# X tiles loaded in one row, a reciprocal in the gate chain, and two forms of the first output row moved in a two-layer decoder kernel

## The reference

```python
y = rmsnorm(x, a_norm)
proj = y @ w_in                                   # q, k, v, o and 2*4 gate columns
gates = 15.0 * tanh((gates + b_gates) / 15.0)
ig, fg = split(gates)
lf = log_sigmoid(fg)
# per head, in chunks: b = cumsum(lf); D = b_t - b_s + ig_s; running maximum m
# num = (q k^T * exp(D - m)) v + exp(...) C q ; h = num / max(|den|, exp(-m))
x = x + (rmsnorm(h) * sigmoid(o)) @ w_out
x = x + swiglu(rmsnorm(x))                        # w_gate_up, w_down
# second layer: shared K/V, sliding-window attention with sinks, then swiglu; final rmsnorm
```

## Time and profile before

| | |
|---|---|
| median of three runs | 2072.8 us (2071.33 to 2073.25) |
| the profiled execution | 2074.34 us, its span 2072.7 us |
| PE busy in the span | 2019.2 us (97%) |
| DVE, ACT, POOL busy | 1349.9, 925.3, 1211.6 us |
| granted PE clock, mean | 0.994 |
| moved by DMA | 415.03 MB, 200 GB/s |

### The profile page before, as it was taken

How to read it: one execution, slowest core, us unless ns; L and a number is a source line. 1 busy time by engine, 2 the same in 40 slices (tenths; PEclk the granted TensorE clock), 3 DMA queues, 4 the chain that set the end, 5 groups by cost and what they waited for, 6 DMA issues and landing times.

```text
span 2072.7 us, 29248 instructions
## 1 busy us (share of the span) xinstructions
PE 2019.2 (97%) x9992; PEld 1660.2 (80%) x9992; DVE 1349.9 (65%) x1929; ACT 925.3 (45%) x1951; POOL 1211.6 (58%) x1058
## 2 busy tenths in 40 slices
PE   7899999999999999999999999899999999999998
PEld 6788989878888888888878666588788888888886
DVE  7654652668777777464665677768776676645567
ACT  6444343365545545432344444536545444432233
POOL 5532520664888988565664111264888797756565
PEclk9999999999999999999999999999999999999999
DMA  5655545843777787795844000564567667688673
GB/s 154 194 189 181 184 156 203 304 133 122 254 234 258 238 255 244 252 393 169 269 136 85 28 22 22 203 213 122 176 231 251 226 229 249 213 306 313 203 257 139
DMA packets 295431, 415.03 MB, mean 200 GB/s; under 512 B 40040, under 2 KB 218232, under 8 KB 295296
## 3 DMA queue, kind: packets, MB, share of 16 engines
q1 hardware_dynamic: 260752, 307.87, 45.3%
q10 hardware_dynamic: 33120, 100.68, 13.5%
q0 software_dynamic: 1424, 4.77, 0.8%
HBM read 259.09 MB, written 154.17 MB: 199 GB/s over the span
## 4 chain that ended last, share of the span: by engine, by line
PE 86%; DVE 7%; ACT 3%; issue 2%; DMA 1%; POOL 0%; SPq 0%; ACTq 0%; DVEq 0%; POOLq 0%
PE ps L2216 21%; PE ps L2218 21%; PE ps L2217 21%; PE ps L2119 8%; PE ps L2121 4%; PE ps L2480 1%; PE ps L2339 1%; PE ps L2340 1%; PE ps L2336 1%; PE ps L2271 1%; PE ps L2509 1%; DVE mats L1652 1%; PE ps L2499 1%; DVE forms L1750 1%; PE ps L2385 1%
## 5 line engine op out<-in xcount | busy, mean ns | idle before, releaser
L2216 PE MATMUL ps<-forms,mats 128*128 128x512 f32 x2016 | 789.6, 392 | 5.5 <-ACT part L1302 2.3
L2218 PE MATMUL ps<-forms,mats 128*128 128x512 f32 x2016 | 785.9, 390 | 0.0
L2217 PE MATMUL ps<-forms,mats 128*128 128x512 f32 x2016 | 785.8, 390 | 0.0
L1007 POOL TENSOR_TENSOR mats<-sum_a,mats 128x256 fp32r<-128x256 f32 (+2 forms) x384 | 405.6, 1061 | 365.4 <-ACT mats L1241 364.4
L2216 PEld LDWEIGHTS ps<-forms,mats 128*128 128x128 f32 x2016 | 379.4, 188 | 90.8 <-issue 10.2
L2218 PEld LDWEIGHTS ps<-forms,mats 128*128 128x128 f32 x2016 | 379.3, 188 | 79.2
L2217 PEld LDWEIGHTS ps<-forms,mats 128*128 128x128 f32 x2016 | 379.5, 188 | 77.6
L1675 DVE TENSOR_TENSOR X<-ps,X 128x512 f32<-128x512 f32 x390 | 268.4, 690 | 218.4 <-PE ps L2218 216.1
L1241 ACT ACTIVATE mats<-sum_a 128x256 fp32r<-128x256 f32 (+2 forms) x392 | 201.6, 516 | 324.0 <-PE ps L2218 306.7
L1652 DVE TENSOR_TENSOR mats<-stream_raw,mats 128x256 fp32r<-128x256 f32 (+2 forms) x302 | 277.1, 919 | 18.7 <-ACT mats L1241 18.0
L1241 ACT ACTIVATE mats<-stream_raw 128x256 fp32r<-128x256 f32 (+2 forms) x302 | 156.6, 519 | 249.6 <-PE ps L2218 246.1
(11 more groups left out here) (230 smaller groups left out, 2696.2 us busy)
## 6 DMA issues: line engine op xcount, KB each, us to landing
forms<-scratch_forms ACTq DMA_DIRECT2D x182, 512.0 KB, 5.4
scratch_forms<-prep_forms SPq DMA_DIRECT2D x161, 512.0 KB, 3.5
stream_raw<-in_w_gate_up_dram SPq DMA_DIRECT2D x88, 512.0 KB, 5.4
scratch_forms<-head_forms SPq DMA_DIRECT2D x49, 512.0 KB, 2.6
scratch_hidden<-hidden SPq DMA_DIRECT2D x84, 256.0 KB, 5.5
prep_raw<-in_w_down_dram SPq DMA_DIRECT2D x38, 512.0 KB, 5.7
stream_raw<-scratch_hidden SPq DMA_DIRECT2D x32, 512.0 KB, 4.6
forms<-scratch_forms SPq DMA_DIRECT2D x28, 512.0 KB, 8.1
```

The source lines that it names most:

```text
L1007: pool.tensor_tensor(blocks(m[:, q, 1, :], it.width), stream_source(it, q), blocks(m[:, q, 0, :].bitcast(F32), it.width), ALU.subtract).th ...
L2216: mm(dst, ah, bh, start=OPENS[q] and k == 0, stop=False, skip_group_check=True)
L2217: mm(dst, ah, bl, start=False, stop=False, skip_group_check=True)
L2218: m = mm(dst, al, bh, start=False, stop=k == w - 1, skip_group_check=True)
```

## The change

Three groups of edits, all in the first 130 us.

1. SP loads the eight x tiles in one row, and the norm's weights behind them. The two transfers of gate columns are issued by ACT's queue before its first instruction. The gate unit's split stands one tile earlier in the lists of ACT and DVE (behind tile 2's transposes in place of tile 3's).
2. In the gate chain, 1/u comes from a DVE reciprocal of 4x1024 in place of ACT's exp(-ln u). ACT scales the input gate, behind its logarithm and a one-column Exp that brings its table back. The hi part of head 0's unit 3 is made before the logarithm. POOL gains unit 4 behind the lo part of unit 3 and unit 5 behind the reload of the first row.
3. In head 0, ACT makes no form behind value copy 5; forms 5 and 6 of the first row stand behind copies 6 and 7, and the lo part of form 6 goes from before the chunk loop to its first turn.

```diff
@@ SP
-            for t in range(3):
+            for t in range(TT):
                 load_x(t)
-            sp.wait_ge(gate_w_cleared, 1)
-            ... (two gate column transfers)
-            load_gains(0, a_norm[0, :])
-            for t in range(3, TT):
-                load_x(t)
+            sp.dma_start(gcol[:, 0, :], a_norm[0, :].rearrange("(k p) -> p k", p=P), ...
+                         ).then_inc(a_gain_loaded, 16)
@@ POOL
-            for j in range(3, 6):
-                gain(Unit(U_HEADS + j))
+            gain(Unit(U_HEADS + 3))
...
+            gain(Unit(U_HEADS + 4))
             pool.wait_ge(gate_dve, 10)
             pool.dma_start(scr_negm, negm[:]).then_inc(negm_stored, 16)
             pool.wait_ge(negm_stored, 16)
             load_neg_row(0)
+            gain(Unit(U_HEADS + 5))
@@ ACT
+            act.wait_ge(gate_w_cleared, 1)
+            act.dma_start(gates[:, :, 0:NH_A], win[:, :, g0:g0 + NH_A]).then_inc(gate_w_loaded, 16)
+            act.dma_start(gates[:, :, 32:32 + NH_A], win[:, :, g0 + NH_A:g0 + 2 * NH_A]).then_inc(gate_w_loaded, 16)
-                if t == 5:
+                if t == 4:
                     write_hi(Unit(U_GATES))
...
-            act.wait_ge(gate_dve, 3)
+            write_hi(Unit(U_HEADS + 3))
+            act.wait_ge(gate_dve, 2)
             act.activation(lnu[:], one_enf[:], ACT.Ln).then_inc(gate_act, 1)
-            act.wait_ge(gate_act, 2)
-            act.activation(fg[:], lnu[:], ACT.Exp, scale=-1.0).then_inc(gate_act, 1)
-            write_hi(Unit(U_HEADS + 3))
+            act.activation(table_col[:], neghalf[:, 0:1], ACT.Exp)
+            act.activation(ig[:], ig[:], ACT.Copy, scale=GATE_CAP).then_inc(gate_act, 1)
...
-                        if first and t < NQ:
-                            head_row_hi(0, t)
+                        if first and t != 5:
+                            head_row_hi(0, t - t // 6)
@@ DVE
-                if t == 5:
+                if t == 4:
                     write_lo(Unit(U_GATES))
...
-            dve.wait_ge(bank_free[5], K[5] + 1)
-            dve.tensor_scalar(ig[:], ig[:], GATE_CAP, None, ALU.mult).then_inc(gate_dve, 1)
...
+            dve.reciprocal(fg[:], one_enf[:]).then_inc(gate_dve, 1)
...
-                    for q in range(3, NQ):
+                    for q in range(3, NQ - 1):
                         head_row_lo(0, q)
...
-                    if first and c:
-                        head_row_lo(1, c - 1)
+                    if first:
+                        head_row_lo(int(c > 0), (c - 1) % NQ)
```

More of the change, by code:

```diff
@@ L650, in load_gains @@
                 sp.dma_start(gcol[:, i, :], g.rearrange("(k p) -> p k", p=P), allow_slow_non_contiguous=True
-                             ).then_inc(a_gain_loaded if i == 0 else gains_loaded, 16)
-            for t in range(3):
+                             ).then_inc(gains_loaded, 16)
+            for t in range(TT):
                 load_x(t)
-            sp.wait_ge(gate_w_cleared, 1)
[L656 to L659, removed]
-            load_gains(0, a_norm[0, :])
-            for t in range(3, TT):
-                load_x(t)
+            sp.dma_start(gcol[:, 0, :], a_norm[0, :].rearrange("(k p) -> p k", p=P), allow_slow_non_contiguous=True
+                         ).then_inc(a_gain_loaded, 16)
             load_head(0, 0, range(2))
@@ L1389, in run @@
                     tile_hi(2, 3, 1)
+            act.wait_ge(gate_w_cleared, 1)
+            gates = raw[:, 0, :].rearrange("p (k n) -> p k n", k=KT)
+            g0 = 2 * NH_A * DQK + 2 * D
+            act.dma_start(gates[:, :, 0:NH_A], win[:, :, g0:g0 + NH_A]).then_inc(gate_w_loaded, 16)
+            act.dma_start(gates[:, :, 32:32 + NH_A], win[:, :, g0 + NH_A:g0 + 2 * NH_A]).then_inc(gate_w_loaded, 16)
             K = uses.stage(NORM)
@@ L1844, in _ @@
             write_lo(Unit(U_HEADS + 2))
-            K = uses.stage(BANK_45)
-            dve.wait_ge(bank_free[5], K[5] + 1)
-            dve.tensor_scalar(ig[:], ig[:], GATE_CAP, None, ALU.mult).then_inc(gate_dve, 1)
+            uses.stage(BANK_45)
             dve.wait_ge(gate_act, 1)
             dve.tensor_scalar(one_enf[:], enf[:], 1.0, None, ALU.add).then_inc(gate_dve, 1)
-            dve.wait_ge(gate_dve, 3)
+            dve.wait_ge(gate_dve, 2)
             dve.scalar_tensor_tensor(enf[:], one_enf[:], -1.0, enf[:], ALU.add, ALU.subtract
                                      ).then_inc(gate_dve, 1)
+            dve.reciprocal(fg[:], one_enf[:]).then_inc(gate_dve, 1)
             dve.wait_ge(gate_dve, 4)
-            dve.wait_ge(gate_act, 3)
             dve.tensor_tensor(enf[:], enf[:], fg[:], ALU.mult).then_inc(gate_dve, 1)
             dve.wait_ge(gate_dve, 5)
+            dve.wait_ge(gate_act, 2)
             dve.tensor_tensor(lf[:], enf[:], lnu[:], ALU.subtract).then_inc(gate_dve, 1)
@@ L1862, in _ @@
                                    ).then_inc(gate_dve, 1)
+            dve.wait_ge(gate_act, 3)
             dve.tensor_tensor_scan(mrow[:], lf[:], ig[:], 0.0, ALU.add, ALU.max
```

## The result

The changed kernel takes 2078.61 us (median of 8 runs, 2075.66 to 2079.39) against 2073.03 us of the kernel before (8 runs beside it, 2071.33 to 2075.25): ratio 1.0025, 95% interval 1.0016 to 1.0035. That is 5.6 us slower, outside the range of 2068.6 to 2077.6, and it was forecast as no change. Run again with the experiments it took 2078.17 us, ratio 1.0023 (1.0014 to 1.0032). The profiled execution took 2078.45 us with a span of 2076.8, 4.1 us more than before.

What follows compares the result with a forecast made beforehand. PE, busy 97% of the span, was taken as the bound, so only its waits could be won. The terms 2.0 + 0.0 + 0.3 - 1.7 gave +0.6 us: 2074.9 against 2073.4, no change, range 2068.6 to 2077.6.

Steps and rivals of the forecast that it cites:

- Edit 1, +2.0: Start: weights behind tile 7 delay the gate unit and x_normed of tile 7; +2.0 us, ends 0 and +2.5.
- the even sharing of the queues: Start: gate columns' small packets go one to one with X's, so gate columns and X both land near 15.7.
- PE's transposes of tile 7 and all that follows shift by +2.0: Start: x_normed of tile 7 at 25.6 instead of 23.62 passes to PE and everything behind it as +2.0 us.
- Edit 2, 0.0 and +0.3: Gate chain ends where it did, 0.0 us (-3.0 to +1.6); POOL's gain of unit 5 ahead of e_inter's store, +0.3.
- R: Gate chain: duration of DVE's reciprocal of 1024 elements, taken as 6.8 us; break-even 6.75, ends 1.2 and 8.4.
- PE's wait of 2.68 us stays: Gate chain: with its end unmoved, PE's wait before the transposes of gate_stack remains 2.68 us.
- Edit 3, -1.7: First head: chunk 1 starts at 93.8 for 96.24, -2.4 us, of which 0.7 is given back; ends -2.9 and 0.
- the state after it comes some 0.7 us late: First head: form 6's later lo part delays row 1's load, landing about 101; the state after chunk 2's den slips 0.7 us.
- dear: Rival, gate chain: reciprocal of 8.4 us, PE's wait before gate_stack's transposes grows to 4.3; +2.2, 2075.0 us; chance 0.16.
- cheap reciprocal: Rival, gate chain: one-pass reciprocal of 1.2 us, chain 3.0 shorter, PE's 2.68 us wait gone; 2070.4 us; chance 0.26.
- starving columns: Rival, start: gate columns on ACT's queue lose against SP's, gate unit at 19.7; +4.6, 2077.4 us; chance 0.12.
- Edit 3 gives nothing: Rival, first head: the clock falls in PE's new wait, so edit 3 gains nothing; +2.3, 2075.1 us; chance 0.12.

Runs made afterwards that it cites:

- e9: Changed kernel with the gate unit's split back at tile 5's turn in ACT's and DVE's lists, loads as in the changed kernel: 2075.38 us, ratio 1.0015.
- e10: Changed kernel with 40 identity transposes on PE ahead of tile 4's transposes and 17 ahead of tile 5's: 2077.81 us, ratio 1.0028.
- e4: Changed kernel with SP issuing X tiles 0 to 4, gate columns, norm's weights, then tiles 5 to 7: 2074.43 us, ratio 1.0005.
- e7: Changed kernel with form 6's lo part back ahead of the chunk loop, value copies as in the changed kernel: 2074.71 us, ratio 1.0006.
- e11: Kernel before with the third edit's value copies, form 6's lo part left where it was: 2070.01 us against 2072.63, ratio 0.9988.

## Why the prediction was wrong

**Edit 1, +2.0, was +4.25 at T0.** Everything up to x_normed of tile 7 came as worked out (15.93 for 15.7, 18.37 for 18.2, 25.72 for 25.6), the even sharing of the queues included. The step that failed is "PE's transposes of tile 7 and all that follows shift by +2.0". It put PE's own way to tile 7 at nothing. Tile 7 was normed 2.0 us later than before (27.54 against 25.53), as forecast, but PE reached it only at 29.87, 2.3 us after that, where before it had taken it up at once. Two things together made this: the split ahead of tile 5, which took PE's 0.9 us in hand, and the low clock behind the wait of 4.37 us, by which PE's work between tiles 5 and 7 took 7.39 us for 5.27. The prediction named the earlier split for ACT, and followed it to tile 7, which has the split ahead of it before and after; it didn't look at tile 5. The clock was weighed for edit 3's wait and left out for the start's wait, which was twice as long. So of the 4.25 us 2.0 are tile 7's own delay and 2.2 the low clock with nothing in hand. e9 takes away the one condition and e10 the other, and in both T0 is back at 8.7 to 8.8 us behind tile 7. Tile 7's own delay comes from the weights for the most part: with them sooner (e4) it is normed 2.8 us sooner, and the split's turn moves it by 0.35 (e9 against e10, whose gains both start at 16.02).

**Edit 2, 0.0 and +0.3, was -0.45.** Right, and so was the way to it: R = 6.53 us for 6.8. "PE's wait of 2.68 us stays": it was 2.23. The Trainium skill, "VectorE: DVE Perf Modes", section "First, the fixed hardware budget", has a repeat count of 8 for the reciprocal's divide; eight passes would have been 8.3 us as an estimate, and the measured 6.53 decides.

**Edit 3, -1.7, was +0.33.** Less the 3.8 us by which all was late, its times stood as worked out: first state written at 93.3, load issued at 94.7 (94.4), landed at 101.1 (101). The step that failed is "the state after it comes some 0.7 us late". DVE stood 6.37 us for the form of row 1 with chunk 2's den behind it in its list, and PE paid 3.1 us in two waits, 1.75 at chunk 3, for the state that chunk 2 leaves, and 1.32 at 117.3. The sum from the rows: -2.7 (v_one), +1.3 and +3.1 (C_state), +0.2 (SwT), -1.7 (the clock of the earlier trace rows, now 1.00), together +0.2. That the price hangs on the lo part alone is shown by e7 and e11.

**The rivals.** The dear and the cheap reciprocal are both out by the row. The starving columns are out: the weights landed on time. "Edit 3 gives nothing" was the case, with another reason than the one named, which was the clock. Only the starving rival put a loss at the start, for the reason just ruled out; slower by over 0.2%, which is what came (0.25%), had the chance of 0.17. Behind H, where the prediction would have PE's waits change by no more than a microsecond, PE's idle time went from 35.8 to 37.1 us in a stretch of the same length, which is no part of the loss. Of the 5.6 us of the medians the marks explain 4.1; the other 1.5 is within the intervals and not assigned.

## What to carry to other kernels

Two things can hold an engine at a hand-over: the piece that it is fed, and its own work since the last one. Follow a shift along both. Between tiles 5 and 7 the chain left PE 6.16 us before and 5.12 after, and PE's own work takes 5.27 at full clock and took 7.39 with the clock low; the chain alone gave +2.0, the second gave the other 2.2. The 0.9 us between 6.16 and 5.27 is what PE had in hand. When a list's order changes by one turn, write down what now stands *ahead* of the next hand-over on every engine that has the piece; 1.2 us of DVE work moved across one x_normed cost 2.5 us at T0 with the clock low behind it (38.47 against 35.99), and 0.4 with the clock kept up (e10's 36.42 against 35.99). And before a piece is moved behind a result, ask which transfer starts at its end: form 6's lo part took 0.7 us and held a load of 6.3.

## What the runs showed of the hardware

- DVE's reciprocal takes 6.53 us for 4x1024 elements, 6.4 ns for each of the 1024, against 1.21 us for a tensor operation of the same form. Its small forms (154 and 164 ns in the earlier trace rows) hardly show it.
- Packets of 16 bytes on one queue went one for one with 4 KB packets on another (10 to 12 us, changed kernel), and took 6.3% of the engines' time (all 16) while doing so:

```profile
q1 hardware_dynamic: 216, 0.79, 98.8%
q10 hardware_dynamic: 216, 0.00, 6.3%
```

- The granted clock came back to the upper level only at 27.0 us in the changed kernel, over 7 us after PE had started again at 19.18, with PE still waiting 1.33 us in between. With work in both gaps it never fell. What the low clock cost hung on what PE had in hand: 2.1 us in the changed kernel, nothing at T0 in the kernel before and in the one with the split at tile 5, where PE took up tile 7 as soon as it was normed. In the kernel with the second edit alone PE waited 2.1 us for v_one and the clock stayed at 1.00 from 90 to 95; before it waited 2.7 us and the same window had 0.66. G to H was 68.52 us against 70.70: a wait 0.6 us shorter, and 2.2 us. With the first edit alone PE waited 2.7 us for v_one as before, and the window behind it (95 to 100) again had 0.66. These are one profile each.
